# The triangular inverse of the first mixer in three steps that quadruple the blocks, with pairs of level masks added, instead of six that double them

## What is computed

```
def gated_delta_rule(q, k, v, g, beta):
    ...
    a = jnp.where(strict, jnp.einsum("bhncd,bhnjd->bhncj", k_beta, k) * decay, 0.0)
    eye = jnp.eye(CHUNK, dtype=jnp.float32)
    t_inv = lax.linalg.triangular_solve(eye + a, jnp.broadcast_to(eye, a.shape),
                                        left_side=True, lower=True)
    u = jnp.einsum("bhncj,bhnjv->bhncv", t_inv, v_beta)
    ...
```

## Time and profile before

| | |
|---|---|
| median of 3 executions | 1490.23 us (1489.03 to 1490.94) |
| the profiled execution | 1488.6 us, span 1487.0 us |
| mean granted TensorE clock | 0.985 of full speed |
| stretch of the first mixer's four groups | about 70 to 352 us of the span |

### The profile page before, as it was taken

The page is one execution under the profiler, slowest core; times in us unless marked ns, Lnnn a source line. Parts: engine busy times, 40 slices in busy tenths (PEclk is TensorE's granted clock), DMA queues, the critical chain, the costliest instruction groups (busy, mean ns, idle before and its releaser), DMA issues.

```text
span 1487.0 us, 19983 instructions
## 1 busy us (share of the span) xinstructions
PE 1429.9 (96%) x7838; PEld 1214.4 (82%) x7838; DVE 938.5 (63%) x1654; ACT 734.3 (49%) x1246; POOL 18.5 (1%) x43
## 2 busy tenths in 40 slices
PE   6899999999999999999999999999999998999998
PEld 5798989888888888988888878778888876888887
DVE  5667776765765555757555479876555487565553
ACT  5653545433454443655444356655444465454441
POOL 3010000000000000000000000000000000000000
PEclk9999999999999999999999999999999997999999
DMA  9322323222566554526665536326665451266652
GB/s 264 86 71 72 100 59 86 70 71 72 171 199 186 185 191 139 177 86 196 183 186 184 188 124 199 127 65 205 186 187 190 160 170 58 91 197 187 186 189 85
DMA packets 168108, 216.60 MB, mean 146 GB/s; under 512 B 11009, under 2 KB 136272, under 8 KB 167888
## 3 DMA queue, kind: packets, MB, share of 16 engines
q1 hardware_dynamic: 166832, 213.03, 46.2%
q10 hardware_dynamic: 1184, 2.31, 0.5%
HBM read 214.26 MB, written 1.05 MB: 145 GB/s over the span
## 4 chain that ended last, share of the span: by engine, by line
PE 77%; DVE 16%; ACT 4%; issue 2%; DMA 2%; DVEq 0%; ACTq 0%; SPq 0%
PE psum L878 20%; PE psum L880 20%; PE psum L879 20%; DVE w_low L627 4%; PE psum L1139 3%; PE psum L1134 2%; PE psum L1071 2%; PE psum L1250 2%; PE psum L1226 2%; PE psum L1187 1%; DVE work L2224 1%; PE psum L1053 1%; ACT w_high L613 1%; PE psum L1239 1%; DVE work L799 1%
## 5 line engine op out<-in xcount | busy, mean ns | idle before, releaser
L627 DVE TENSOR_TENSOR w_low<-ring,w_high 128x1024 fp32r<-128x1024 f32 (+3 forms) x395 | 474.2, 1210 | 327.6 <-ACT w_high L613 325.7
L613 ACT ACTIVATE w_high<-ring 128x1024 fp32r<-128x1024 f32 (+3 forms) x395 | 411.3, 1048 | 449.7 <-PE psum L880 431.8
L878 PE MATMUL psum<-w_high,hT 128*128 128x512 f32 (+2 forms) x944 | 372.7, 395 | 0.6 <-DVE hT L2031 0.6
L880 PE MATMUL psum<-w_high,hT 128*128 128x512 f32 (+2 forms) x944 | 366.9, 389 | 0.0
L879 PE MATMUL psum<-w_low,hT 128*128 128x512 f32 (+2 forms) x944 | 366.3, 388 | 0.0
L878 PE MATMUL psum<-w_high,parts 128*128 128x512 f32 (+1 forms) x532 | 208.1, 391 | 0.4 <-DVE work L2563 0.4
L880 PEld LDWEIGHTS psum<-w_high,hT 128*128 128x128 f32 x944 | 177.6, 188 | 36.7
L878 PEld LDWEIGHTS psum<-w_high,hT 128*128 128x128 f32 x944 | 178.1, 189 | 34.9 <-DVE hT L2031 0.9
L880 PE MATMUL psum<-w_high,parts 128*128 128x512 f32 (+1 forms) x532 | 206.0, 387 | 0.0
L879 PEld LDWEIGHTS psum<-w_low,hT 128*128 128x128 f32 x944 | 178.1, 189 | 33.9
L879 PE MATMUL psum<-w_low,parts 128*128 128x512 f32 (+1 forms) x532 | 205.8, 387 | 0.0
(11 more groups left out here) (274 smaller groups left out, 1514.8 us busy)
## 6 DMA issues: line engine op xcount, KB each, us to landing
ring<-in_ffn_w_gate_up SPq DMA_DIRECT2D x176, 256.0 KB, 3.2
ring<-in_w_gate_up SPq DMA_DIRECT2D x176, 256.0 KB, 3.2
ring<-in_gdn_w_in SPq DMA_DIRECT2D x48, 512.0 KB, 3.8
ring<-in_ffn_w_down SPq DMA_DIRECT2D x44, 512.0 KB, 3.3
ring<-in_w_down SPq DMA_DIRECT2D x44, 512.0 KB, 3.3
ring<-in_da_w_qkv SPq DMA_DIRECT2D x24, 512.0 KB, 3.9
ring<-in_gdn_w_out SPq DMA_DIRECT2D x16, 512.0 KB, 3.3
ring<-in_mla_w_out SPq DMA_DIRECT2D x8, 512.0 KB, 3.9
```

Source lines behind the costliest of these rows:

```text
L613: nc.scalar.activation(piece_slot(w_high, n), piece_slot(ring, n), ACT.Copy).then_inc(s.w_hi, 1)
L627: nc.vector.tensor_tensor(piece_slot(w_low, n), piece_slot(ring, n), piece_slot(w_high, n).bitcast(F32), ALU.subtract).then_inc(s.w_lo, 1)
L878: mm(out, lhs[0], rhs[0], start=start, stop=False)
L880: return mm(out, lhs[1], rhs[0], start=False, stop=stop)
```

## The change

Three steps of four blocks take the place of six levels of two. In step `step` (0, 1, 2) the diagonal blocks of n = 2, 8, 32 rows are joined by fours. The mask of a step is the sum of the masks of levels 2*`step`+1 and 2*`step`+2; GpSimd adds the three pairs once at the start, and three masks are transposed instead of six. With P the masked product (`g_p`) and Y the inverse so far, the joined inverse is Y - PY + P(PY): TensorE multiplies P by the last three of each four blocks of Y (96 columns), VectorE subtracts that from Y, TensorE multiplies P by the last two blocks of the result (64 columns), ScalarE copies that to `g_w` (which lies in `g_x`), TensorE multiplies P by `g_w` (64 columns), and VectorE adds the product to the last two blocks of Y. `beside_level` of the odd level stands between the second and the third of these rounds, that of the even level after the transposes. `squares_kq` of the next group writes over the place of `g_x`, and waits for the last round of step 2 instead of the first round of level 6.

```diff
-STEPS = 2 * (LEVELS - 1)
+STEPS = (LEVELS - 1) // 2
...
+        def g_w(t):
+
+            return g_x[:, t, 0:GH // 2, :].rearrange("p q (e n) -> p (q e) n", e=2)
+
...
-        def level_mask(n, heads):
-
-            return const("level")[:, n * P:(n + 1) * P].unsqueeze(1).to_broadcast([P, heads, P])
+        def masks_of(at, heads):
+
+            return const("level")[:, at * P:(at + 1) * P].unsqueeze(1).to_broadcast([P, heads, P])
 
...
-        def g_step(g, lv, t):
-
-            return g * STEPS + 2 * lv + t + 1
-
-        def half_of(v, lv, odd):
-
-            n = 1 << lv
+        def g_step(g, step, t):
+
+            return (g * STEPS + step) * T + t + 1
+
+        def later_blocks(v, step, first):
+
+            n = 2 << (2 * step)
             if len(v.shape) == 2:
-                return v.rearrange("p (b two n) -> p b two n", two=2, n=n)[:, :, odd, :]
-            return v.rearrange("p h (b two n) -> p h b two n", two=2, n=n)[:, :, :, odd, :]
-
-        def packed(bank, lv):
-
-            return bank[:, 0:GH * P // 2].rearrange("p (h b n) -> p h b n", h=GH, n=1 << lv)
+                return v.rearrange("p (b m) -> p b m", m=4 * n)[:, :, first * n:4 * n]
+            return v.rearrange("p h (b m) -> p h b m", m=4 * n)[:, :, :, first * n:4 * n]
+
+        def packed(flat, step, first):
+
+            n = 2 << (2 * step)
+            cols = P * (4 - first) // 4
+            return flat[:, 0:GH * cols].rearrange("p (h b m) -> p h b m", h=GH, m=(4 - first) * n)
 
...
-                pe.wait_ge(s.consts_loaded, 16)
-                for n in range(1, LEVELS):
-                    last = nc.tensor.transpose(B[2 + (n - 1) // 4][:, (n - 1) % 4 * P:(n - 1) % 4 * P + P],
-                                               const("level")[:, n * P:(n + 1) * P], ident)
+                pe.wait_ge(s.steps_summed, 1)
+                for step in range(STEPS):
+                    last = nc.tensor.transpose(B[2][:, step * P:(step + 1) * P], const("level")[:, (2 * step + 1) * P:(2 * step + 2) * P], ident)
                 last.then_inc(s.mask_psum, 1)
 
...
+            def inverse_step(g, step):
+
+                def each_head(t, rhs, of_bank, ready, done):
+                    pe.wait_ge(ready, g_step(g, step, t))
+                    for h in range(GH):
+                        last = mm(of_bank(B[t])[:, h], g_p[:, t, h, :], rhs(t, h), start=True, stop=True)
+                    last.then_inc(done, 1)
+
+                for t in range(T):
+                    pe.wait_ge(s.gx_ready, g_step(g, step, t))
+                    for h in range(GH):
+                        last = mm(B[t][:, h * P:(h + 1) * P], g_at[:, t, h, :], g_x[:, t, h, :], start=True, stop=True)
+                    last.then_inc(s.p_psum, 1)
+                for t in range(T):
+                    each_head(t, lambda t, h: later_blocks(g_y[:, t, h, :], step, 1), lambda bank: packed(bank, step, 1), s.p_ready, s.q_psum)
+                for t in range(T):
+                    each_head(t, lambda t, h: later_blocks(g_y[:, t, h, :], step, 2), lambda bank: packed(bank, step, 2), s.less_ready, s.w_psum)
+                beside_level(g, 2 * step + 1)
+                for t in range(T):
+                    each_head(t, lambda t, h: g_w(t)[:, h, :], lambda bank: bank[:, 0:GH * P // 2].rearrange("p (h n) -> p h n", h=GH),
+                              s.w_ready, s.r_psum)
 
                 for t in range(T):
-                    turned_y(g, 0, t)
-                for lv in range(1, LEVELS):
-                    for t in range(T):
-                        pe.wait_ge(s.gx_ready, g_step(g, lv - 1, t))
-                        for h in range(GH):
-                            last = mm(B[t][:, h * P:(h + 1) * P], g_at[:, t, h, :], g_x[:, t, h, :], start=True, stop=True)
-                        last.then_inc(s.p_psum, 1)
-                    for t in range(T):
-                        pe.wait_ge(s.p_ready, g_step(g, lv - 1, t))
-                        for h in range(GH):
-                            last = mm(packed(B[t], lv)[:, h, :, :], g_p[:, t, h, :], half_of(g_y[:, t, h, :], lv, 1), start=True, stop=True)
-                        last.then_inc(s.q_psum, 1)
-                    if lv < LEVELS - 1:
+                    turned_y(g, t)
+                for step in range(STEPS):
+                    inverse_step(g, step)
+                    if step < STEPS - 1:
                         for t in range(T):
-                            pe.wait_ge(s.gy_ready, g_step(g, lv - 1, t))
-                            turned_y(g, lv, t)
-                    beside_level(g, lv)
-
-                pe.wait_ge(s.gy_ready, g_step(g, LEVELS - 2, 1))
+                            pe.wait_ge(s.gy_ready, g_step(g, step, t))
+                            turned_y(g, t)
+                    beside_level(g, 2 * step + 2)
+
+                pe.wait_ge(s.gy_ready, g_step(g, STEPS - 1, 1))
                 pe.wait_ge(s.vt_ready, 4 * g + 4)
                 heads(0, lambda h: g_y[:, 0, h, :], lambda h: g_vt[:, 0, h, :], s.u_psum)
...
                 if g:
-                    act.wait_ge(s.p_psum, g_step(g - 1, LEVELS - 2, 1))
+                    act.wait_ge(s.r_psum, g_step(g - 1, STEPS - 1, 1))
...
-            def copy_x(g, lv):
-
-                for t in range(T):
-                    act.wait_ge(s.gx_psum, g_step(g, lv, t))
+            def copy_x(g, step):
+
+                for t in range(T):
+                    act.wait_ge(s.gx_psum, g_step(g, step, t))
                     f(g_x[:, t, :, :].rearrange("p h n -> p (h n)"), B[t][:, :], ACT.Copy).then_inc(s.gx_ready, 1)
+
+            def copy_w(g, step):
+
+                for t in range(T):
+                    act.wait_ge(s.w_psum, g_step(g, step, t))
+                    f(g_w(t).rearrange("p h n -> p (h n)"), B[t][:, 0:GH * P // 2], ACT.Copy).then_inc(s.w_ready, 1)
 
...
-                for lv in range(1, LEVELS):
-                    if lv < LEVELS - 1:
-                        copy_x(g, lv)
-                    beside_level(g, lv)
+                for step in range(STEPS):
+                    copy_w(g, step)
+                    beside_level(g, 2 * step + 1)
+                    if step < STEPS - 1:
+                        copy_x(g, step + 1)
+                    beside_level(g, 2 * step + 2)
...
-            v.tensor_copy(const("level")[:, P:5 * P], B[2][:, :])
-            v.tensor_copy(const("level")[:, 5 * P:7 * P], B[3][:, 0:2 * P]).then_inc(s.mask_ready, 1)
+            v.tensor_copy(const("level")[:, P:(1 + STEPS) * P], B[2][:, 0:STEPS * P]).then_inc(s.mask_ready, 1)
...
-                for lv in range(1, LEVELS):
+                for step in range(STEPS):
                     for t in range(T):
-                        dve.wait_ge(s.p_psum, g_step(g, lv - 1, t))
-                        tt(g_p[:, t, :, :], by_head(B[t][:, :]), level_mask(lv, GH), ALU.mult).then_inc(s.p_ready, 1)
+                        dve.wait_ge(s.p_psum, g_step(g, step, t))
+                        tt(g_p[:, t, :, :], by_head(B[t][:, :]), masks_of(1 + step, GH), ALU.mult).then_inc(s.p_ready, 1)
                     for t in range(T):
-                        dve.wait_ge(s.q_psum, g_step(g, lv - 1, t))
-                        yt = half_of(g_y[:, t, :, :], lv, 1)
-                        tt(yt, yt, packed(B[t], lv), ALU.subtract).then_inc(s.gy_ready, 1)
-                    beside_level(g, lv)
+                        dve.wait_ge(s.q_psum, g_step(g, step, t))
+                        yt = later_blocks(g_y[:, t, :, :], step, 1)
+                        tt(yt, yt, packed(B[t], step, 1), ALU.subtract).then_inc(s.less_ready, 1)
+                    beside_level(g, 2 * step + 1)
+                    for t in range(T):
+                        dve.wait_ge(s.r_psum, g_step(g, step, t))
+                        yt = later_blocks(g_y[:, t, :, :], step, 2)
+                        tt(yt, yt, packed(B[t], step, 2), ALU.add).then_inc(s.gy_ready, 1)
+                    beside_level(g, 2 * step + 2)
 
                 more = g + 1 < GROUPS
                 dve.wait_ge(s.u_psum, g * 2 + 1)
...
             pool.wait_ge(s.consts_loaded, 16)
+            doubled = const("level")[:, P:LEVELS * P].rearrange("p (step two n) -> p step two n", two=2, n=P)
+            tt(doubled[:, :, 0, :], doubled[:, :, 0, :], doubled[:, :, 1, :], ALU.add).then_inc(s.steps_summed, 1)```

TensorE's list, the first level and the start of the second in group 0, where no projection tile stands between them. In it `psum<-consts,work` x8 is `turned_y`, the row of 128x128 on `work` the product with `g_x`, the narrower rows the products with `g_p`, and `psum<-consts,arena` x8 is `turned_v` of `beside_level(g, 1)`. Before:

```order
L1053 MATMUL psum<-consts,work 128x128 x8
L1134 MATMUL psum<-work 128x128 x8
L1139 MATMUL psum<-work 128x64 x8
L1053 MATMUL psum<-consts,work 128x128 x8
L1046 MATMUL psum<-consts,arena 128x128 x8
L1134 MATMUL psum<-work 128x128 x8
L1139 MATMUL psum<-work 128x64 x8
```

(11 more changed lines are left out.)

## The result

The changed kernel takes 1464.82 us (median of 5 executions, 1463.53 to 1469.03) against 1490.23 before (median of 5, 1486.75 to 1491.08); the ratio is 0.9831, with a 95% interval of 0.9818 to 0.9844. So it is 25.4 us faster. Measured twice more, beside other kernels, it took 1467.6 and 1467.7 with before at 1491.0 and 1492.4, ratios of 0.985 and 0.983; these two times lie inside the range.

A forecast was written before the change was run, and what follows sets the result against it. TensorE, busy for 96% of the span, was taken as the bound, with its waits for VectorE. Savings of 14.0 + 2.2 + 0.5 + 1.4 = 18.1 from 1490.2 gave 1472.1 us, range 1466.5 to 1477.

The forecast's parts named there:

- The transposes, 14.0: Transposes on TensorE: six rounds per group become three, at 1.17 each over 4 groups, 14.0 us saved.
- No wait before the second and third rounds: Handoffs inside a step: the 384-element subtraction and ScalarE's copy end in time for the `g_p` rounds, cost 0.
- the rival of slow handoffs: Two extra handoffs per step, 24 in all at 0.35 each, give back 8.4 us: 1480.5; chance 0.07.
- the one of a late copy of `g_w`: ScalarE's copy comes late behind a whole `beside_level`, 1.8 at each of 12 places: 1493.7, slower than before; chance 0.03.
- The product rounds. Sum 0: Twelve product rounds per group stay twelve, and 64, 96 and 128 columns take about 1.83 to 1.84 each: no change.
- the rival of cheaper narrow rounds: Product rounds of 64 columns cost 0.92 and of 96 columns 1.38, 5.6 more saved: 1466.5; chance 0.03.
- The waits for VectorE, 2.2 + 0.5 + 1.4: Shorter TensorE waits: 2.2 saved between levels in four groups, 0.5 at level 2, 1.4 before `heads` in groups 1 and 2.
- I take both losses as kept: Clock losses behind waits, 2.6 in group 1 and 1.6 in group 3, stay; bounds 4.2 less to 2.6 more.
- The rival that had the clock stay up: The clock stays up behind the waits in the groups, 4.2 us more saved: 1467.9; chance 0.16.
- The start, 0: Start of the program, with fewer mask transposes and copies: taken as 0, between 0 and 0.5 us saved.
- the first `turned_y` of group 2: Sign in the profile: group 2's first `turned_y` comes some 9.6 us earlier, 5.0 more than group 1's 4.1.

The follow-up runs named there:

- six masks: Changed kernel with the start as before, six masks transposed and copied back instead of three: 1464.60 us, ratio 0.9829.
- query products first: Changed kernel with VectorE's query products ahead of the low parts of two weight pieces beside level 1: 1464.56 us, ratio 0.9821.
- the two kernels with the query products first: Changed kernel with that move alone, 1464.56 us, and with a weight piece's low part and the decays' masking also moved later, 1459.33 us.
- the longer waits: Changed kernel with VectorE's masking of the next group's decays done twice, so TensorE waits longer before `heads`: 1471.25 us, ratio 0.9868.

## Why the prediction was right in direction and too small

- **The transposes, 14.0: right.** They take 1.17 a round where nothing waits, three rounds a group are gone, and the kernel that leaves them out of before shows the gain with VectorE's list whole. Only level 3's, which a projection tile follows, took 1.09 and not 1.17 (171.22 to 172.31 in group 1), so the term should have been 13.7.
- **No wait before the second and third rounds: right.** Both run without one, and the rival of slow handoffs and the one of a late copy of `g_w` fall. The subtraction of 384 elements takes 0.55 to 0.56.
- **"The product rounds. Sum 0": too small by 2.0.** The 96 columns cost as much as 64 or 128, so the rival of cheaper narrow rounds falls. The prediction read the Trainium skill, "TensorE: Matmul & The Clock Gate", section "Back-to-back issue gap", by its table of columns, which is for matmuls by themselves; for a stream of weight loads and matmuls the same section says that the spacing is set by both. With that the rows agree better, 1.83 and 1.84 for 64 and 128 columns. What I missed is the first weight load of a round. Before, each narrow round's weights were `g_p` written just ahead, and its first load and first matmul start at the same time (190.15 in level 5 of group 1). In the changed kernel only the first of the three rounds has such weights; for the others they lie ready, and the third's first load starts at 149.00, its first matmul at 149.12. So the first two take 3.62 instead of 3.68, and the third 1.73 instead of 1.84: 12 x (0.06 + 0.11) = 2.0. The 0.11 lies at the start: the second matmul record of the round follows the first by 0.16 before and by 0.06 in the third round, and the others follow 0.11 apart in both. That the load is the reason is read from the rows and was not tried by itself.
- **The waits for VectorE, 2.2 + 0.5 + 1.4: right in place and nearly in size.** The one before step 1's transposes costs 2.87 - 1.73 = 1.14 (forecast 1.25), the one before `heads` 3.04 - 1.73 = 1.31 (1.46). Two additions in a row take 0.74 where I counted 0.84.
- **"I take both losses as kept": the step that failed most.** The falls of the clock in groups 1 and 2 became rarer and shorter. In before they came in three of four stretches, at 2.6 to 2.8 a stretch, and in two of six of the changed kernel, at 1.35. That is 4.0 per execution before and 0.9 after, 3.1 less, an estimate from two and three profiles. The one profile that the forecast was read from showed 2.6 and not 4.0. In group 3 the clock falls in every profile of both, as I took it. The rival that had the clock stay up was the nearer one. That shorter waits would make the falls rarer stood in the prediction, but no term of the sum had it.
- **The start, 0: right in the mean, but 1.8 in the two profiles compared.** The six masks show that it isn't the masks.
- **A slip:** the first `turned_y` of group 2 was forecast some 9.6 us earlier; by the prediction's own terms it is 4.1 + 5.0 = 9.1. The sum doesn't use it.

Apart from the falls in groups 1 and 2, the groups gained 4.6 + 5.6 + 5.6 + 4.4 = 20.2, against 18.1 forecast; the difference is mostly the 2.0 of the product rounds. With the clock, 20.2 + 3.1 = 23.3, which would have given 1466.9. The three medians put the gain at 25.4, 23.4 and 24.8; what is over 23.3 lies within the spread of single executions, and I don't attribute it.

**The clock by the waits' length.** All idle times of TensorE of 0.7 us or more in the stretch of the groups (75 to 356 us), over the twelve profiles, and in how many cases the granted clock began to fall in them or within 3 us behind them (those under 0.7 us show one such fall, behind a wait of 0.51 that follows one of 1.26):

| idle time, us | where | falls |
|---|---|---|
| 0.73 to 1.12 | 37 places, most of them 0.8 ahead of a tile or 0.97 before step 1's transposes | 0 of 37 |
| 1.14 to 1.16 | before `heads` in groups 1 and 2 of the changed kernel, six masks, query products first | 3 of 10, at 1.35 us |
| 1.26 to 1.53 | levels 4 and 6 of before, group 3 of the two kernels with the query products first, one tile | 5 of 11 |
| 2.04 to 3.29 | `heads` with the longer waits, group 3 of all other kernels | 12 of 12 |

The Trainium skill, "TensorE: Matmul & The Clock Gate", section "Part 1: The HAM clock gate (the "warmup" mystery)", says that idleness lets the clock fall, and the counts agree with that. The one experiment that only lengthened a wait agrees too. But at the same length some executions fall and some don't, and what else decides, these runs don't show. The waits of 0.51 that stand behind those of 1.26 in before did not start the fall in two of its three cases: in group 1 the granted clock was 0.50 at 201.90 to 202.20, ahead of the end of that wait at 202.71. Whether they make it longer is open, since no kernel had one of the two alone.

## What to carry to other kernels

When an algorithm can be written with more work per step and fewer steps, count the rounds on the engine that bounds: here twelve rounds of products stayed twelve, and it was the transposes between the steps that went. Waits on the bounding engine can cost more than their length: behind those of 2.04 us and more its clock fell each time, behind those of 1.14 to 1.53 in 8 of 21, and a fall cost 1.3 us or more. Price them with that, as a chance per execution, and profile each kernel more than once before a difference of 2 us is read as an effect. A wait for another engine's list goes away if work is moved to a place where that engine idles, and only moves on if it is put in front of the next thing that is waited for.

## What the runs showed of the hardware

- A round of eight float32 products with a weight load for each (16 records) takes 1.73 to 1.84 us for 64, 96 and 128 columns alike. With 64 columns it took 1.84 where the weights were written just ahead and 1.73 where they lay ready.
- The granted clock fell at 12 of 12 idle times of TensorE of 2.04 to 3.29 us, at 8 of 21 of 1.14 to 1.53 and at none of 37 of 0.73 to 1.12.
- Behind a wait of 2.86 us three such rounds took 9.87 instead of 5.57, with the granted clock at the lower of its two levels (1.2 GHz) for part of it.
- The same program reached group 0 at 67.99, 69.00 and 72.38 us in three executions.
